# Gated recurrence and delta rule: one after the other, or queued woven into each other

## The reference, cut to what matters

```python
y = concatenate([
    short_conv_mixer(p_conv, ...),   # y columns 0..255:    3 taps, gated
    hgrn2_mixer(p_hg, ...),          # y columns 256..639:  gated recurrence, 6 heads of 64
    rwkv7_mixer(p_rw, ...),          # y columns 640..1023: delta rule, 6 heads of 64
])
h = h + y @ w_mix_out
# gated recurrence:  state = exp(lf_t) * state + k_t v_t ;  o_t = q_t state ; rms norm per head, gate
# delta rule:        state = state * w_t + (state a_t) b_t + v_t k_t ;  y_t = state r_t ; group norm, bonus, gate
```

## Time and profile before

| | us |
|---|---|
| median of 3 executions | 4246.5 (4243.03 to 4251.54) |
| the profiled execution | 4253.05 |
| its span, first to last instruction | 4251.2 |
| from the barrier of `mixer` to the first matmul of `w_mix_out`, layer 0 | 308.8 to 629.1 |
| the same in layer 1 | 1262.4 to 1582.0 |

### The profile page before, as it was taken

One profiled execution on the slowest core, in us unless ns is written; L12 is line 12 of the kernel. 1 busy time (PEld: TensorE's weight loads), 2 busy tenths in 40 slices (PEclk: granted clock), 3 DMA queues, 4 the chain that ended last, 5 costly groups with the idle time before them and its releaser, 6 DMA issues.

```text
span 4251.2 us, 52431 instructions
## 1 busy us (share of the span) xinstructions
PE 3426.9 (81%) x19980; PEld 2701.8 (64%) x19980; DVE 2893.2 (68%) x3403; ACT 1163.8 (27%) x1503; POOL 413.8 (10%) x453
## 2 busy tenths in 40 slices
PE   7985579999984579998677999999339668888864
PEld 7983458899983468997454676767128554544432
DVE  7865457888865457886655777777373667777755
ACT  1002110100002110101221555656010235665642
POOL 0000100010000100010000121211000011111110
PEclk9996779999996789999897999999669979999987
DMA  5552123344552123452011999999422149999973
GB/s 209 188 185 93 72 97 139 139 179 181 192 200 82 69 100 139 149 189 89 20 40 40 376 369 362 360 359 353 166 99 102 57 173 347 341 347 337 341 266 123
DMA packets 112847, 815.30 MB, mean 192 GB/s; under 512 B 26432, under 2 KB 27456, under 8 KB 40640
## 3 DMA queue, kind: packets, MB, share of 16 engines
q1 hardware_dynamic: 78768, 726.75, 46.1%
q0 software_dynamic: 32768, 83.96, 5.6%
q10 hardware_dynamic: 1040, 1.05, 0.1%
HBM read 809.03 MB, written 56.10 MB: 204 GB/s over the span
## 4 chain that ended last, share of the span: by engine, by line
PE 60%; DVE 27%; ACT 7%; issue 3%; DMA 3%; POOL 0%; DVEq 0%; SPq 0%; POOLq 0%; ACTq 0%
PE ps L364 40%; PE ps L1682 15%; DVE ring_r L1679 7%; DVE arena L396 4%; DVE arena L404 3%; DVE ring_r L128 2%; PE ps L1705 1%; ACT arena_hi L1678 1%; DVE arena L400 1%; ACT ring_r L1678 1%; DMA arena<-yd_dram 1%; ACT arena L412 1%; DVE ring_r L127 1%; DVE arena L439 1%; DVE arena L1737 1%
## 5 line engine op out<-in xcount | busy, mean ns | idle before, releaser
L364 PE MATMUL ps<-arena_r,ring_r 128*128 128x256 f32 (+1 forms) x10224 | 1314.0, 290 | 88.2 <-DVE arena_r L396 36.6
L364 PEld LDWEIGHTS ps<-arena_r,ring_r 128*128 128x128 f32 x10224 | 1271.0, 191 | 129.3 <-issue 28.8
L1682 PE MATMUL ps<-ring_r,arena_r 128*128 128x512 f32 x1720 | 543.0, 415 | 9.3 <-DVE ring_r L1679 9.3
L412 ACT ACTIVATE arena<-arena 128x256 f32<-128x256 f32 (+4 forms) x288 | 141.4, 491 | 1393.3 <-DVE arena L396 990.0
L128 DVE TENSOR_TENSOR ring_r<-ring,ring_r 128x4096 fp32r<-128x4096 f32 x115 | 509.0, 4426 | 3.9
L1682 PE MATMUL ps<-ring,arena 128*64 128x512 f32 (+1 forms) x1064 | 481.9, 596 | 1.8 <-DVE arena L1757 1.8
L364 PE MATMUL ps<-arena 128*128 128x128 f32 (+5 forms) x2364 | 356.8, 330 | 129.7 <-DVE arena L396 58.5
L1679 DVE TENSOR_TENSOR ring_r<-ring,arena_hi 128x2048 fp32r<-128x2048 f32 x156 | 357.6, 2293 | 103.0 <-ACT arena_hi L1678 83.2
L364 PEld LDWEIGHTS ps<-arena 128*128 128x128 f32 (+1 forms) x2364 | 290.9, 220 | 201.3 <-DVE arena L396 87.9
L1682 PEld LDWEIGHTS ps<-ring_r,arena_r 128*128 128x128 f32 x1720 | 338.6, 199 | 85.6 <-DVE ring_r L1679 10.4
L127 DVE CAST ring_r<-ring 128x4096 fp32r<-128x4096 f32 x115 | 291.7, 2537 | 68.6 <-PE ps L364 58.9
(11 more groups left out here) (165 smaller groups left out, 3132.8 us busy)
## 6 DMA issues: line engine op xcount, KB each, us to landing
ring<-wexp_dram SPq DMA_DIRECT2D x399, 1024.0 KB, 8.2
ring<-stream_dram SPq DMA_DIRECT2D x145, 2048.0 KB, 7.7
arena<-yd_dram POOLq DMA_DIRECT2D x12, 2048.0 KB, 7.6
xd_dram<-arena POOLq DMA_DIRECT2D x6, 512.0 KB, 3.0
consts_sb<-consts_dram SPq DMA_DIRECT2D x1, 2241.5 KB, 9.8
arena<-xd_dram,small POOLq DMA_INDIRECT x133, 7.0
yd_dram<-arena,small POOLq DMA_INDIRECT x133, 8.4
arena<-mem_dram POOLq DMA_DIRECT2D x2, 1024.0 KB, 6.9
```

Source lines behind the costliest of these rows:

```text
L364: return PE(lambda e: e.matmul(ps, lhsT=lhsT, rhs=rhs, start=start, stop=stop, skip_group_check=True), *after, inc=inc)
L412: return ACTQ(lambda e: e.activation(out_, a, f, bias=bias, scale=scale), *after, **kw)
L1682: return P(lambda e: e.matmul(out_, lhsT=x, rhs=y, start=st_, stop=sp_, skip_group_check=True), *after, inc=inc)
```

## The change

`hgrn` and `rwkv` become generators that yield at named points, and `upto` runs one of them to its next point. `mixer` alternates between them, so their instructions stand mixed in the queues. In front of the inverse stand the convolution (behind the logarithms of the recurrence), the preparations of both, and levels 8, 7 and half of 6. Each of the 18 steps of the inverse is followed by one piece of the recurrence (a half level b, or a piece of the output) and half a piece of the modulation. There are no barriers between the three mixers. The delta rule keeps its buffers in the idle part of the ring (`spare`) and in parts of the arena that are free. In `hgrn` the three Sigmoids stand together. The rms norm and the group norm are done once over 768 elements rather than twice over 384. The splitting of the first `w_mix_out` chunk is issued behind the group norm's transposes rather than ahead of it. Y(0) to Y(4) are split behind the inverse and Y(5) to Y(7) at the end. 34 pieces of the modulation stand ahead of the first inverse level, 3 in it, 9 in the inverse, 12 in the chain, and 3 behind it.

```diff
-    def prepare(self):
+    def prepare(self, *after):

         c = len(self.specs) // CH
         assert len(self.specs) % CH == 0 and not self.plain
         if c not in self.ahead:
-            self.split(c)
+            self.split(c, after)

...
+            def __init__(self, base, n, of=None):
+                assert base + n <= (NA if of is None else of.shape[1]), (base, n, NA)
+                self.base, self.n, self.of = base, n, arena if of is None else of

             def v(self, o=0, n=None):
                 n = self.n - o if n is None else n
                 assert o + n <= self.n
-                return arena[:, self.base + o:self.base + o + n]
+                return self.of[:, self.base + o:self.base + o + n]
...
-            FILL.start(modulation(l, f) if stop >= 9 else iter(()))
-
-            Z = Reg(wk, 520)
+            mm(MF[0:1, 0:1], con("col"), con("col"), True, True, f, wa)
+            FILL.start(modulation(l, f))
+            spare = ring[:, NSLOT * CH * 128:(NSLOT + NHI) * CH * 128]
+
+            ha = hgrn(l, P, Y, wk, f)
+            upto(ha, "logs")
+            Z = Reg(6144, 520, spare)
             z = Z.t(260)
             t = DVE(lambda e: e.memset(Z.v(0, 520), 0.0), f)
             t = tt(DVE, z[:, :, 2:258], P(2, 2).rearrange("p (k w) -> p k w", w=256), P(4, 2).rearrange("p (k w) -> p k w", w=256), ALU.mult)
-            T = Reg(wk + 520, 512)
+            T = Reg(6144 + 520, 512, spare)
             for j in range(2):
                 tj = T.v(256 * j, 256)
                 ts(DVE, tj, z[:, j, 0:256], par("conv_w", l, j), par("conv_b", l, j), ALU.mult, ALU.add)
                 stt(tj, z[:, j, 1:257], par("conv_w", l, 2 + j), tj, ALU.mult, ALU.add)
                 stt(tj, z[:, j, 2:258], par("conv_w", l, 4 + j), tj, ALU.mult, ALU.add)
-                tt(DVE, Y(j), tj, P(j), ALU.mult)
-            f = barrier()
-            hgrn(l, P, Y, wk, f)
-            f = barrier()
-            rwkv(l, P, Y, Pr, wk, W2, G2, wa, f)
+                tconv = tt(DVE, Y(j), tj, P(j), ALU.mult)
+            rb = rwkv(l, P, Y, Yr, wk, W2, G2, wa, spare, [f, tconv])
+            FILL.step(4)
+            upto(rb, "mixed")
+            FILL.step(4)
+            upto(ha, "scanned")
+            upto(rb, "gates")
+            FILL.step(6)
+            upto(ha, "gates")
+            upto(rb, "scanned")
+            FILL.step(6)
+            upto(ha, "turned")
+            upto(rb, "keys")
+            FILL.step(6)
+            upto(rb, "bonus")
+            upto(ha, "level")
+            upto(rb, "hats")
+            FILL.step(4)
+            upto(ha, "level")
+            upto(rb, "turned")
+            FILL.step(4)
+            for g in range(3):
+                upto(rb, "first")
+                upto(ha, "level")
+                FILL.step(1)
+            for i in range(18):
+                upto(rb, "inverse")
+                upto(ha, "level")
+                FILL.step(0.5)
+            upto(ha, "end")
+            YH = Reg(22528, 2048)
+            yh = Halves(Y, lambda k: YH.v(256 * k, 256))
+            got_a = PE.mark()
+            for k in range(5):
+                yh.make(k, got_a)
+            upto(rb, "end")
             f = barrier()
             B.banks = psb
-            YH = Reg(wk, 2048)
-            yh = Halves(Y, lambda k: YH.v(256 * k, 256))
-            for k in range(KT):
+            for k in range(5, KT):
                 yh.make(k, f)

...
+
+            tk = act(Fl, Fl, ACT.Sigmoid, tscan, scale=-1.0)
+            tq = act(T2.v(), Q, ACT.Sigmoid)
+            tg = act(GG.v(), Gt, ACT.Sigmoid)
             if l == 1:
...
-            FILL.step(4)
-            t = times(8, decays(8))
+            te = decays(8)
+            yield "level"
+            t = times(8, te)
             for lev in range(8, 0, -1):

                 if lev > 1:
@@ -747,13 +792,14 @@
                 else:
                     kq = XL[0]
                     tdiag = cp(DVE, kq.v(), Fl, left_x.get(0))
-                scores(XL[lev % 2], XL[lev % 2], lev, t, acc, ATT, A0, T1, left_x)
+                yield from scores(XL[lev % 2], XL[lev % 2], lev, t, ATT, A0, left_x)
                 if lev > 1:
                     t = times(lev - 1, te)

-            scores(kq, None, 0, tdiag, acc, ATT, A0, T1, left_x, Q)
+            yield from scores(kq, None, 0, tdiag, ATT, A0, left_x, Q)
...
+                t = cp(DVE, OT.v(384 * b, 384), ps[:, 0:384], t)
+                B.leave(ps, t)
+            yield "level"
+            s12 = small[:, 24:36]
+            tt(DVE, T1.v(), OT.v(), OT.v(), ALU.mult)
+            DVE(lambda e: e.tensor_reduce(s12, v3(T1.v(), 64), AX.X, ALU.add))
+            t = ts(DVE, s12, s12, 1.0 / 64, 1e-6, ALU.mult, ALU.add)
+            t = power(s12, -0.5, t)
+            yield "level"
+            t = tt(DVE, v3(OT.v(), 64), v3(OT.v(), 64), v3(s12, 1).broadcast_to([128, 12, 64]), ALU.mult, t)
+            for b in range(2):
                 ps, w = B.take()
                 for j in range(3):
-                    t = tr(ps[:, 128 * j:128 * j + 128], ob[:, 128 * j:128 * j + 128], w, t, inc=j == 2)
+                    tk = tr(ps[:, 128 * j:128 * j + 128], OT.v(384 * b + 128 * j, 128), w, t, inc=j == 2)
                 g3 = GG.t(256)[:, :, 128 * b:128 * b + 128]
                 y3 = v3(Y(2, 3), 256)[:, :, 128 * b:128 * b + 128]
-                t = tt(DVE, y3, v3(ps[:, 0:384], 128), g3, ALU.mult, t)
-                B.leave(ps, t)
-
...
-                FILL.step(1)
-            left_x[lev % 2] = PE.mark()
-
-        def rwkv(l, P, Y, Pr, wk, W2, G2, wa, f):
-            o8 = 8192
-            LW, E, A, G, KK, BON = [Reg(o8 + 768 * i, 768) for i in range(6)]
-            T1, EM = Reg(4096, 768), Reg(4096 + 768, 768)
-            YT = Reg(2048, 768)
-            G3 = [[Reg(wk + 2048 * g + 512 * i, 512) for i in range(4)] for g in range(3)]
-            DD = Reg(wk, 11 * 256)
+                if b:
+                    left_x[lev % 2] = PE.mark()
+                yield "level"
+
+        def rwkv(l, P, Y, Yr, wk, W2, G2, wa, spare, f):
+            A, LW = Reg(2048, 768), Reg(2048 + 768, 768)
+            E, G = Reg(8192, 768), Reg(8192 + 768, 768)
+            KK, BON = Reg(Yr.base + 1280, 768), Reg(wk, 768)
+            YT = E
+            T1, EM = Reg(6144, 768, spare), Reg(6144 + 768, 768, spare)
+            G3 = [[Reg(2048 * g + 512 * i, 512, spare) for i in range(4)] for g in range(3)]
+            DD = Reg(0, 11 * 256, spare)
...
-                FILL.step(1)
+                yield "first"
             xdone = {g: (DVE, DVE.n) for g in range(3)}
-            CT = [Reg(2048 + 768, 512), Reg(o8 - 2048, 512), Reg(o8 - 1536, 512)]
+            CT = [Reg(7680, 512, spare), Reg(2048 + 1536, 512), Reg(6400, 512)]
             cdone = {}
...
-                    FILL.step(1)
+                    yield "inverse"
...
             FILL.finish()
             W.mode(False)
-            W.prepare()
             got_y = PE.mark()
+            m12, q12 = small[:, 52:64], small[:, 192:204]
+            m12b = v3(m12, 1).broadcast_to([128, 12, 64])
+            q12b = v3(q12, 1).broadcast_to([128, 12, 64])
+            y12, tmp = v3(YT.v(), 64), A.v()
+            DVE(lambda e: e.tensor_reduce(m12, y12, AX.X, ALU.add), got_y)
+            ts(DVE, m12, m12, 1.0 / 64, None, ALU.mult, None)
+            tt(DVE, y12, y12, m12b, ALU.subtract)
+            tt(DVE, tmp, YT.v(), YT.v(), ALU.mult)
+            DVE(lambda e: e.tensor_reduce(q12, v3(tmp, 64), AX.X, ALU.add))
+            t = ts(DVE, q12, q12, 1.0 / 64, 64e-5, ALU.mult, ALU.add)
+            t = power(q12, -0.5, t)
+            t = tt(DVE, y12, y12, q12b, ALU.mult, t)
+            bk = []
             for b in range(2):
-                yb = YT.v(384 * b, 384)
-                m6, q6 = small[:, 52:58], small[:, 58:64]
-                tmp = T1.v(0, 384)
-                m6b = v3(m6, 1).broadcast_to([128, 6, 64])
-                q6b = v3(q6, 1).broadcast_to([128, 6, 64])
-                DVE(lambda e, yb=yb: e.tensor_reduce(m6, v3(yb, 64), AX.X, ALU.add), got_y)
-                ts(DVE, m6, m6, 1.0 / 64, None, ALU.mult, None)
-                tt(DVE, v3(yb, 64), v3(yb, 64), m6b, ALU.subtract)
-                tt(DVE, tmp, yb, yb, ALU.mult)
-                DVE(lambda e, tmp=tmp: e.tensor_reduce(q6, v3(tmp, 64), AX.X, ALU.add))
-                t = ts(DVE, q6, q6, 1.0 / 64, 64e-5, ALU.mult, ALU.add)
-                t = power(q6, -0.5, t)
-                t = tt(DVE, v3(yb, 64), v3(yb, 64), q6b, ALU.mult, t)
                 ps, w = B.take()
                 for j in range(3):
-                    t = tr(ps[:, 128 * j:128 * j + 128], yb[:, 128 * j:128 * j + 128], w, t, inc=j == 2)
-                for j in range(3):
+                    tk = tr(ps[:, 128 * j:128 * j + 128], YT.v(384 * b + 128 * j, 128), w, t, inc=j == 2)
+                bk.append((ps, tk))
+            W.prepare(got_y)
+            for j in range(3):
```

(19 more changed lines are left out.)

61 lines of the change are left out of this document (27 added, 34 removed).

## The result

The changed kernel takes 4271.0 us (median of 6 runs) against 4248.7 of the kernel before beside it, 1.0047 times as long, 95% interval 1.0036 to 1.0058: about 20 us slower. One of the six took 8251.2 us and is left out of the ratio; the median of the other five is 4270.0. The prediction was 4256.8 us, slower, in a range from 4217 to 4290. The profiled execution has 4273.7 us and a span of 4271.9.

A forecast was written before the change was run, and what follows sets the result against it. No engine bounds the mixers for long; a TensorE and ScalarE chain paces the inverse. Woven gains of 5.0 and 1.3 against losses of 4 and 4.3 a layer gave 10.3 us slower: 4263.4, less 6.5, 4256.8 (4217 to 4290).

The forecast's parts named there:

- parts 1 and 2: Woven inverse: levels moved into it take 106.6 us at full clock, against 136.6 and 132.9 us for both stretches before.
- The two kinds of steps: Woven inverse: second-half steps take 4.9 us; first-half steps take 7.7, TensorE waiting 2.7 for VectorE's `times`.
- The 106.6 us at the full clock: Woven inverse: its summed length per layer if TensorE is granted 2.4 GHz throughout.
- part 4: Woven inverse: GpSimd's mask holds up VectorE's `times` and `decays` in five steps, 3 us of 0 to 7.
- part 3: Woven inverse: TensorE holes lower the clock, a 0.3 share at 1.2 GHz costing 22 us a layer.
- The prediction's upper bound of 45 us: Woven inverse: most clock loss, from the earlier levels' clock 0.69, about 0.6 of the time low.
- rival (c): Woven inverse: clock stays low in most of it, 42 us lost for 22, total 4297; chance 0.16.
- rival (a): Woven inverse: clock holds, loss 6 for 22 and little contention, total 4221, faster; chance 0.22.
- part 5: Front: hidden convolution gains 5 us, VectorE's waits behind modulation clusters cost more; 4 us lost, bounds +6 to -10.
- the two of 6 that I named: Front: sign that VectorE idles about 6 us twice between the gates and the first inverse.
- Rival (b): Front: it gains 10 us a layer as the streams fill each other's waits, total 4237; chance 0.12.
- part 6: End: splits lose 3.2 us, chain pieces 5.5, the single norm saves 4.4; 4.3 lost a layer, bounds 1 to 8.

The follow-up runs named there:

- e1: Changed kernel with GpSimd's mask of CT in the inverse waiting for VectorE's woven work of three steps back: 4241.8 us, 0.9980 of the kernel before.
- e2: Changed kernel with ten useless matmuls on TensorE ahead of each first half of levels 5 to 1: 4243.2 us, 0.9982 of the kernel before.
- e3: Changed kernel with the two `times` and the next subtraction queued half a step earlier on VectorE: 4190.6 us, 0.9861 of the kernel before.
- e5: Changed kernel with smaller modulation clusters, fewer pieces in the front and the recurrence's gates and transposes following at once: 4243.8 us, 0.9975 of the kernel before.
- e4: Changed kernel with only the front woven, the recurrence's levels and output queued ahead of the first inverse level: 4208.1 us, 0.9898 of the kernel before.
- e7: Changed kernel with the splitting of Y(0) to Y(4) moved back behind the last barrier: 4263.5 us, 1.0028 of the kernel before.
- e9: Changed kernel with the inverse unwoven, smaller modulation clusters and Y split at the end: 4194.0 us, 0.9873 of the kernel before.
- e10: Changed kernel with `times` half a step earlier and smaller modulation clusters, Y(0) to Y(4) still split ahead of the masks: 4151.4 us, 0.9790.

## Why the prediction was right in direction and half in size

- **Bound and direction (parts 1 and 2).** The two kinds of steps, the hole in every second one and its releaser are as predicted. The 106.6 us at the full clock can't be read from the changed kernel. e1's hole of 2.76 confirms the 2.7 that they rest on.
- **The lock (part 4), mis-sized.** Taken 3 us of 0 to 7; it is 1.1 us in every one of the five steps, 5.5 us, and it hit the path each time. GpSimd starts 0.02 us ahead of the block (446.86 and 446.88), both released by the end of the same addition. The row of before had shown GpSimd first; the value nearest to it was the upper bound. The Trainium skill (SBUF — State Buffer, SBUF: two separate sides) has the rule by which the one that starts first holds the ports; the trace agrees. The masked copies behind them, with one operand in PSUM, take 1.29 us beside GpSimd's mask (442.08 and 442.06), for 1.27 before.
- **The clock (part 3), mis-sized.** This is the larger error. Of the 143.5 us, 106.6 + 5.5 leave 31 for the clock and whatever else is in it, where 22 stood. e2 shows 14 to 17 of it directly. Two reasons can be read from the rows: the holes were 3.85 and not 2.7, and e1 shows that this 1.1 us alone is worth 9 to 12 us of clock in a layer; and the Sqrt's stretch (0.56 for 28 us) had been costed as 6.9 us for a step, without a clock of its own. The prediction's upper bound of 45 us was also worked out wrongly: a clock of 0.69 means 0.6 of the time at 1.2 GHz, but only 0.31/0.69 = 0.45 of the work, and 0.45 of 72 us is 32. That is what was measured: TensorE is busy 105.2 us in the woven stretch for the 72 that the prediction gave it at 2.4 GHz, 33 more. The low clock of the prediction's rival (c), 42 us, lay on the other side of what was measured; rival (a), the clock held, is what e3 comes nearest to (0.91 and 0.88).
- **The front (part 5).** +2.5 and +6.6 around +4: right in size. Of VectorE's four waits the last two (5.94, 6.26) are the two of 6 that I named; the first two (10.82, 6.08) are the gates' and the Sigmoids' behind them, 16.9 us where 10.12 stood. Rival (b) was nearer than its chance said: the same front gains 20 a layer with other clusters (e5), and with the levels run out behind it the mixers gain 23 and 12 (e4).
- **The end (part 6).** Norm 18.4 for 19.4 and 3.3 us of wait at the masks were as named. Halves and chain came to +1.2 and +10.1 around the forecast 8.7, and the clock parts the layers: in layer 0 the chain ran higher than before (0.85 for 0.75), in layer 1 lower (0.73 for 0.87). I had given the chain no clock of its own. The step that failed is that the splits were costed only where they went. Where they had been they gave 3 to 4 us back (e7), and that is most of the 7.7 us of the span that lie outside the mixers.
- **The sum.** Predicted +10.3; measured +20.7: woven stretches 12 and 13 more than predicted, the front +1, the end 8 less (all of it in layer 0), behind the mixers 7 less. That the whole came out slower, as forecast, is in part luck. The woven stretches were to gain 5.0 and 1.3 and lost 6.9 and 12.1; the end was to lose 4.3 a layer and over both layers lost next to nothing. The mechanism that decides, the hole with its lock and clock, was named, but its price was set too low to turn the sign of its own term, and the forecast's loss stood in the front and the end. How near it was shows in e1: without the lock alone the changed kernel is 0.2% faster than the one before.
- **What it should have been compared with.** I set the woven inverse against the sum of the two stretches before and found a small gain. The comparison that decides is between weaving the front alone and weaving both, and it was not made: by it the second half of the change costs 63 us (e4).

## What to carry to other kernels

When two chains are woven into one in-order queue, look at the instruction which the other engine will wait for, and put it at least one of the other chain's latencies ahead of its use: here half a step earlier turned +22 us into -58. A hole on TensorE costs its length and the clock of the work behind it, which here came to as much again or more; filling it with matmuls that nobody reads is a quick way to measure the second part. When work is moved away from a place, cost what its absence gives there as well as what it costs where it goes.

## What the runs showed of the hardware that was not expected

- GpSimd and VectorE, both reading SBUF operands, released by the same instruction: GpSimd was 0.02 us ahead and VectorE's block of three took 3.23 us instead of 2.14 in four steps of a layer, and its block of two 2.24 instead of 1.15 (e1) in the fifth. The other way round, GpSimd's 1.27 us became 2.04 beside VectorE (timeline of the changed kernel):

```profile
556.32 0.96 DVE L396 TENSOR_TENSOR arena<-arena 128x768 f32<-128x768 f32 x1
556.36 2.04 POOL L396 TENSOR_TENSOR arena<-ring,consts_sb 128x512 f32<-128x512 f32 x1 [13.26 <-DVE ring L396]
```

- From 570 to 608 us matmuls without a gap at 1.2 GHz (e5, layer 0), while the same chain ran at 0.85 in the changed kernel and at 0.94 in e7. What decides between them is not settled, and it is not the wait ahead of it alone: in e9, layer 0, TensorE goes into the masks without a wait and the chain runs at 0.62, in e10 it waits 3.71 us there and the chain runs at 0.86.
- Useless matmuls made the kernel 28 us faster (e2).
